# One sum of squares for the final norm of the first block and the first norm of the second, and sums of squares added on GpSimd

## The reference

```python
def rmsnorm(x, g):
    y = x * lax.rsqrt(jnp.mean(x * x, axis=-1, keepdims=True) + EPS)
    return y * g

def first_block(x, ...):
    x = hybrid_layer(x, ...)        # h2 = rmsnorm(x, ln2_g) ahead of its feed-forward part
    return rmsnorm(x, final_g)

def second_block(x, ...):           # rms_norm is the same with NORM_EPS = 1e-5
    h = rms_norm(x, attn_norm_g)
    u = h @ w_in                    # pool part, q, k, v
    ...
    x = x + concat(y_pool, y_diff) @ w_out
    x = x + cross_attention(rms_norm(x, xattn_norm_g), rms_norm(mem, mem_norm_g), ...)
    x = x + moe_ffn(rms_norm(x, ffn_norm_g), ...)       # 32 experts, 4 for a token
    return rms_norm(x, final_norm_g)
```

## Time and profile before

| | |
|---|---|
| median of three runs | 1805.38 us (1804.46 to 1809.14) |
| the profiled execution | 1811.86 us, span 1810.1 us |
| TensorE busy | 1655.3 us, 91% |
| VectorE busy | 733.7 us, 41% |
| ScalarE busy | 482.6 us, 27% |
| GpSimd busy | 153.9 us, 9% |
| DMA, mean over the span | 291 GB/s |
| mean granted clock of TensorE | 0.98 |

### The profile page before, as it was taken

How to read it: one execution, slowest core, us unless ns; L and a number is a source line. 1 busy time by engine, 2 the same in 40 slices (tenths; PEclk the granted TensorE clock), 3 DMA queues, 4 the chain that set the end, 5 groups by cost and what they waited for, 6 DMA issues and landing times.

```text
span 1810.1 us, 22958 instructions
## 1 busy us (share of the span) xinstructions
PE 1655.3 (91%) x9878; PEld 1045.7 (58%) x9878; DVE 733.7 (41%) x1260; ACT 482.6 (27%) x820; POOL 153.9 (9%) x190
## 2 busy tenths in 40 slices
PE   7999999989999899998999988888888888888885
PEld 6998888989999898987333322232323232323221
DVE  5667754677887466745122111111112121212122
ACT  4344454546554344443011000000001010101001
POOL 1200000321552004001000000000000000000000
PEclk9999999999999999999999999999999999999998
DMA  7653322545665452665899999999999999999995
GB/s 203 187 186 106 106 93 93 164 144 171 184 185 180 155 174 78 206 219 189 319 424 422 425 422 424 424 424 423 424 424 425 423 425 424 424 424 425 424 424 230
DMA packets 210202, 525.98 MB, mean 291 GB/s; under 512 B 18121, under 2 KB 135806, under 8 KB 177326
## 3 DMA queue, kind: packets, MB, share of 16 engines
q1 hardware_dynamic: 207104, 519.41, 74.4%
q0 software_dynamic: 2448, 4.82, 1.1%
q10 hardware_dynamic: 542, 0.21, 0.0%
HBM read 523.31 MB, written 1.07 MB: 290 GB/s over the span
## 4 chain that ended last, share of the span: by engine, by line
PE 58%; DMA 35%; DVE 4%; ACT 2%; issue 1%; SPq 0%; POOL 0%; ACTq 0%; DVEq 0%
PE bank L594 57%; DMA slot_ring<-in_w_down 13%; DMA slot_memx<-in_w_down 8%; DMA slot_late<-in_w_down 5%; DMA slot_high<-in_w_down 5%; DMA slot_late<-in_w_gu 1%; DMA slot_last<-in_w_gu 1%; DMA slot_high<-in_w_gu 1%; DVE slot_ring_r L1861 1%; DMA slot_ring<-in_w_in 1%; PE bank L1111 1%; DVE rstd L1900 0%; DVE rot_tmp L2243 0%; ACT high_r L1444 0%; DVE x_sb L1869 0%
## 5 line engine op out<-in xcount | busy, mean ns | idle before, releaser
L594 PE MATMUL bank<-h_hi_r,high_r 128*128 128x256 f32 x1000 | 288.2, 288 | 4.3 <-DVE h_lo_r L1861 4.3
L1861 DVE TENSOR_TENSOR slot_ring_r<-slot_ring,high_r 128x1024 fp32r<-128x1024 f32 x198 | 244.9, 1280 | 101.6 <-ACT high_r L1444 99.3
L594 PE MATMUL bank<-h_lo_r,high_r 128*128 128x256 f32 x1000 | 285.6, 286 | 0.0
L594 PE MATMUL bank<-h_hi_r,slot_ring_r 128*128 128x256 f32 x952 | 271.8, 285 | 0.0
L1865 DVE TENSOR_SCALAR ga<-bank 128x512 f32<-128x512 f32 x32 | 22.1, 692 | 585.1 <-PE bank L594 585.1
L1444 ACT ACTIVATE high_r<-slot_ring 128x1024 fp32r<-128x1024 f32 x198 | 198.0, 1053 | 61.7 <-PE bank L594 43.4
L594 PEld LDWEIGHTS bank<-h_hi_r,high_r 128*128 128x128 f32 x1000 | 193.6, 194 | 5.2 <-DVE h_lo_r L1861 5.0
L594 PEld LDWEIGHTS bank<-h_lo_r,high_r 128*128 128x128 f32 x1000 | 194.0, 194 | 0.1
L1444 ACT ACTIVATE th_e<-ga 128x512 f32<-128x512 f32 x32 | 20.2, 630 | 620.9 <-DVE ga L1865 620.9
L594 PEld LDWEIGHTS bank<-h_hi_r,slot_ring_r 128*128 128x128 f32 x952 | 184.5, 194 | 0.0
L594 PE MATMUL bank<-slot_ring,xg 128*64 128x512 f32 x528 | 124.8, 604 | 12.1 <-DMA slot_ring<-in_w_gu 12.1
(11 more groups left out here) (410 smaller groups left out, 2955.9 us busy)
## 6 DMA issues: line engine op xcount, KB each, us to landing
slot_ring<-in_w_gu SPq DMA_DIRECT2D x66, 1024.0 KB, 22.0
slot_high<-in_w_gu SPq DMA_DIRECT2D x50, 1024.0 KB, 22.1
slot_ring<-in_w_down SPq DMA_DIRECT2D x49, 1024.0 KB, 22.6
slot_last<-in_w_gu SPq DMA_DIRECT2D x38, 1024.0 KB, 22.3
slot_ring<-in_w_in SPq DMA_DIRECT2D x36, 1024.0 KB, 5.0
slot_late<-in_w_gu SPq DMA_DIRECT2D x32, 1024.0 KB, 22.0
slot_high<-in_w_down SPq DMA_DIRECT2D x25, 1024.0 KB, 23.3
slot_ring<-in_w_up SPq DMA_DIRECT2D x44, 512.0 KB, 4.7
```

Source lines behind the costliest of these rows:

```text
L594: return e.matmul(o, lhs, rhs, start=start, stop=stop, skip_group_check=True)
L1861: return e.tensor_tensor(o, i, j, op)
```

## The change

The second norm of the pair takes its sum from squares of x with the gain g1 in the scale, and its gain is g1 g2, so it doesn't wait for the final norm. The final norm is done later: its squares behind memory unit 3, added by GpSimd into one tile, its one sum behind uk 1, its root behind memory unit 4, its products behind the splits for upool. In ln2_g, xattn_g and ffn_g GpSimd adds the squares of pieces 1 and 2 onto piece 0, and TensorE sums pieces 0 and 3 only.

```diff
+        eps_col = {EPS1: small("eps1", 1), EPS2: small("eps2", 1), EPS1 * EPS2: small("eps12", 1)}
+        gain12, gain_sq = small("gain12", KT), small("gain_sq", KT)
...
+        x_sq = tiles(at("x_sq", MIX + (KT + BT) * S, KT * S), KT)
...
...
@@ tensor_program
                 q.wait_ge(*sq_by(norm, i)["square", norm, i])
+                if norm in ADDED:
+                    q.wait_ge(*pool["squares", norm])
...
             def add_residual(w, src, ready, norm):
                 for i in range(4):
                     project((w, i), src, ready, (dve, ("residual", w, i)))
-                    if i:
-                        sums(norm, h, i - 1)
+                sums(norm, h, 0)
                 sums(norm, h, 3)
...
-            pe.mark("final start")
-            for i in range(4):
-                sums("final_g", h, i)
+            pe.mark("block2")
             memory_unit(2)
-            pe.mark("block2")
             for i in range(4):
                 sums("attn_g", h, i)
             memory_unit(3)
...
                 project(("uk", i), hs, h_of("attn_g"), (dve, ("uk", i)))
                 if i:
+                    banks.take(q, ("final_g", "sums"))
+                    q.wait_ge(*pool["squares", "final_g"])
+                    matmul(bank(("final_g", "sums"))[:, 0:S], ones, x_sq[:, 0, :], True, True).then_inc(*pe.step("sums", "final_g"))
+                    banks.give(("final_g", "sums"), (act, ("root", "final_g")))
                     memory_unit(4)
...
+            project(("out2", 2), mix_s, mix_ready, (dve, ("residual", "out2", 2)))
+            project(("out2", 3), mix_s, mix_ready, (dve, ("residual", "out2", 3)))
             sums("xattn_g", h, 0)
-            project(("out2", 2), mix_s, mix_ready, (dve, ("residual", "out2", 2)))
-            sums("xattn_g", h, 1)
-            project(("out2", 3), mix_s, mix_ready, (dve, ("residual", "out2", 3)))
-            sums("xattn_g", h, 2)
             sums("xattn_g", h, 3)
...
@@ gpsimd_program
+            def add_squares(norm):
+                for i in (1, 2):
+                    for j in (0, i):
+                        q.wait_ge(*(act if j % 2 else dve)["square", norm, j])
+                    q.wait_ge(*pool.last())
+                    e.tensor_tensor(h[:, 0:2, :], h[:, 0:2, :], h[:, 2 * i:2 * i + 2, :], ALU.add).then_inc(
+                        *pool.step("squares", norm))
...
             after_all(q, "block2")
+            q.wait_ge(*act["square", "final_g", 3])
+            for n in (4, 2, 1):
+                q.wait_ge(*pool.last())
+                e.tensor_tensor(x_sq[:, 0:n, :], x_sq[:, 0:n, :], x_sq[:, n:2 * n, :], ALU.add).then_inc(
+                    *pool.step("squares", "final_g"))
             q.wait_ge(*dve["pool zero"])
...
             pool.mark("ffn start")
+            add_squares("ffn_g")
+            q.wait_ge(*pool["squares", "ffn_g"])
             for c in range(2):
...
@@ scalar_program
             round_h("ln1_g")
+            q.wait_ge(*dve["gain squares"])
+            af(gain_sq, gain_sq, ACT.Sqrt).then_inc(*act.step("gain root"))
...
-            act.mark("final start")
-            after_all(q, "final start")
-            for i in range(4):
-                squares("final_g", h, x, i, dve["residual", "down", i])
-            sqrt_table()
-            root("final_g", EPS1, "ln2_g")
-            memory_unit(2)
             act.mark("block2")
             after_all(q, "block2")
+            sqrt_table()
             for i in range(4):
-                squares("attn_g", h, x, i, dve["h", "final_g", 2 * i + 1])
-            sqrt_table()
-            root("attn_g", EPS2, "final_g")
+                q.wait_ge(*dve["residual", "down", i])
+                for k in (2 * i, 2 * i + 1):
+                    af(h[:, k, :], x[:, k, :], ACT.Square, scale=gain_sq[:, k:k + 1]).then_inc(*act.step("square", "attn_g", i))
+            memory_unit(2)
+            root("attn_g", EPS1 * EPS2, "ln2_g")
             round_h("attn_g")
             memory_unit(3)
+            for i in range(4):
+                squares("final_g", x_sq, x, i, dve["residual", "down", i])
             for i in range(2):
                 ahead(("uq", i))
                 evac(("uq", i), uq[:, 2 * i:2 * i + 2, :], two_of(("uq", i)), ("uq", i), HD ** -0.5)
                 ahead(("uk", i))
                 if i:
                     memory_unit(4)
+            root("final_g", EPS1, "attn_g")
...
@@ vector_program
             apply("ln1_g", x, h, hs.lo)
+            g1, g2 = (cols_sb[:, col_at[n]:col_at[n] + KT] for n in ("final_g", "attn_g"))
+            tt(gain12, g1, g2, ALU.mult).then_inc(*dve.step())
+            tt(gain_sq, g1, g1, ALU.mult).then_inc(*dve.step())
+            own()
+            ts(gain_sq, gain_sq, EPS2, ALU.add, 1.0 / D, ALU.mult).then_inc(*dve.step("gain squares"))
...
-            dve.mark("final start")
-            q.wait_ge(*act["square", "final_g", 3])
-            apply("final_g", x, x)
-            memory_unit(2)
             dve.mark("block2")
             after_all(q, "block2")
-            q.wait_ge(*act["square", "attn_g", 3])
-            apply("attn_g", x, h, hs.lo)
+            memory_unit(2)
+            apply("attn_g", x, h, hs.lo, gain=gain12)
             memory_unit(3)
...
             for i in range(2):
                 ahead(("upool", i))
+            q.wait_ge(*act["square", "final_g", 3])
+            apply("final_g", x, x)
             for t in two:
                 e.memset(t[:, 0:16], 0.0).then_inc(*dve.step("pool zero"))
```

More of the change, by code:

```diff
@@ L309, in hybrid_moe_program @@
         spare, half_b = small("spare", 1), small("half_b", 32)
-        eps_col = {EPS1: small("eps1", 1), EPS2: small("eps2", 1)}
+        eps_col = {EPS1: small("eps1", 1), EPS2: small("eps2", 1), EPS1 * EPS2: small("eps12", 1)}
+        gain12, gain_sq = small("gain12", KT), small("gain_sq", KT)
         FORGET = sm_at[0]
@@ L399, in hybrid_moe_program @@
         dprob = [area(f"dprob{i}", 384) for i in range(DIFF_H)]
+        assert (DIFF_H + 2) * 384 >= KT * S
+        x_sq = tiles(at("x_sq", MIX + (KT + BT) * S, KT * S), KT)
         assert free[0] <= AR + AREAS - 5 * SLOT
@@ L570, in hybrid_moe_program @@
         MEM_STEPS = ((0, 1), (2, 3), (4, 5), (6, 7), ())
+        ADDED = ("ln2_g", "xattn_g", "ffn_g")
         NORM_START = {"ln2_g": "ln2 start", "xattn_g": "xattn start", "ffn_g": "ffn start"}
@@ L587, in sq_by @@
         def sq_by(norm, i):
-            return act if i % 2 or norm in ("mem_g", "final_g", "attn_g") else dve
+            return act if i % 2 or norm in ("mem_g", "attn_g") else dve
         def tensor_program(e):
@@ L1369, in gpsimd_program @@
             pool.mark("ln2 start")
+            add_squares("ln2_g")
             pool.mark("ff start")
@@ L1380, in gpsimd_program @@
                 ff_split(i)
-            pool.mark("final start")
             pool.mark("block2")
             after_all(q, "block2")
+            q.wait_ge(*act["square", "final_g", 3])
[3 more added lines that the diff above has]
+                    *pool.step("squares", "final_g"))
             q.wait_ge(*dve["pool zero"])
@@ L1405, in gpsimd_program @@
             pool.mark("xattn start")
+            add_squares("xattn_g")
             pool.mark("cross start")
@@ L1894, in squares, with apply @@
                     ALU.mult).then_inc(*dve.step("square", norm, i))
-            def apply(norm, src, dst, lo=None, steps=None):
+            def apply(norm, src, dst, lo=None, steps=None, gain=None):
                 for k in range(KT + 2) if steps is None else steps:
@@ L1902, in apply @@
                     if k < KT:
-                        stt(dst[:, k, :], src[:, k, :], col(norm, k), rstd, ALU.mult, ALU.mult).then_inc(*dve.step("h", norm, k))
+                        stt(dst[:, k, :], src[:, k, :], col(norm, k) if gain is None else gain[:, k:k + 1], rstd, ALU.mult, ALU.mult).then_inc(*dve.step("h", norm, k))
                     if lo is not None and k >= 2:
@@ L1914, in vector_program @@
                 evac(("x", i), x[:, 2 * i:2 * i + 2, :], two_of(("x", i)), ("x", i))
-            for eps in (EPS1, EPS2):
+            for eps in eps_col:
                 e.memset(eps_col[eps], eps).then_inc(*dve.step("eps"))
```

## The result

The changed kernel takes 1796.8 us (median of 5 runs, 1794.4 to 1797.4), the kernel before 1808.6 in the same series (5 runs, 1804.5 to 1813.5): a ratio of 0.9929, interval 0.991 to 0.9947. In a second series they were 1795.6 and 1809.0, 0.9932 [0.9911, 0.9953]. The difference of the medians is 11.9 and 13.4 us where 9.4 was forecast; the profiled span fell by 14.5. (The median of 1805.4 before, from which the forecast counted, came from three runs.)

The account below looks back on a forecast made before the run. Ahead of the expert stage's weight transfers the chain is nearly all TensorE, so instructions taken off it count. 13.7 + 4.8 - 0.5 - 5.2 - 1.8 - 1.6 = 9.4 us gained, 1805.4 to 1796.0; range 1788 to 1803.

Parts of the forecast that it names:

- The join, 28.4 to 14.6: Between block one and two: one sum, two TensorE gaps and a low clock removed; 13.8 us gained, rounded to 13.7.
- under 3 us at clock 1.0: Sign in the join: after down and the memory unit, one sum of 16 taking under 3 us at clock 1.0.
- The later h: At the join's end: h being ready later costs TensorE 0.2 us, taken off the gain.
- The three norms, 4.8: ln2_g, xattn_g, ffn_g: two of four groups of sums dropped each, 5.1 us, cut to 4.8 by collisions in xattn_g.
- The rotation, 5.2 late: Rotation of uk on TensorE waits for ScalarE's squares and VectorE splits taking turns with GpSimd's adds: 5.2 us lost.
- Rival 1: Engines hardly block each other: stall 1.2, no clock drop, softmax 0.8 late; 16.6 us gained, 1788.8. Chance 0.17.
- The low clock, 1.8: After the gap ahead of uk's rotation, TensorE at about half clock for 3.6 us: 1.8 us lost.
- The new sum, 0.5: The final norm's new sum of 2 instructions on TensorE, 0.3 and the slow start: 0.5 us lost.
- The softmax, 1.6 late: VectorE's final-norm reciprocal and products ahead of the first maximum delay the softmax: 1.6 us lost, bounds 0 and 3.5.
- Rival 2: Upper-end costs: softmax 3.5 late, squares 4.4, low clock twice as long; 4.7 us gained, 1800.7. Chance 0.2.
- Rival 3: Expert stage gives back part through differently timed slots; half of 9.4 kept is 1800.7, none 1805.4. Chance 0.1.
- Rival 4: Slower: GpSimd's bias subtractions move behind ffn_g's adds and delay the experts, if 6.7 us each slower by 5.4. Chance 0.05.

Follow-up runs that it names:

- the experiment in which TensorE sums all: Changed kernel without GpSimd's adds of the final norm's squares, TensorE summing 8 products instead of 2: 1798.6 us, 0.9929.
- the pair of experiments: Changed kernel with GpSimd's three final-norm adds held until uk 1 is rotated: 1790.8 us; with ScalarE's four squares moved behind uq 1's split too: 1791.1 us.
- the profile with the wait filled: Changed kernel with 12 float32 matmuls on constants between the rotations of uq 0 and uk 0, output not read: 1794.4 us, 0.9924.
- the reciprocal put on top: Changed kernel with one more VectorE reciprocal (1.75 us) behind the final norm's products, ahead of the softmax: 1798.5 us, 0.9936.
- the squares later: Changed kernel with ScalarE's four final-norm squares moved behind the split of uq 1, GpSimd's adds moving too: 1791.1 us, in another series 1789.8.
- the adds later: Changed kernel with GpSimd's three final-norm adds waiting until VectorE has rotated uk 1, ScalarE's squares staying: 1790.8 us, 0.990.

## Why the prediction was right

**The join, 28.4 to 14.6.** Measured 28.42 to 14.75. From the end of down: squares begin after 4.04 us (4.15 forecast), take 3.29 (2.8), the sum ends after 8.8 (8.6), the reciprocal begins after 10.7 (10.2), uq 0 after 14.75 (14.45, from the prediction's own 615.15 and 629.6; its 14.6 has part of the 0.2 in it that is then taken off once more, and the 13.7 is right to 0.1). ScalarE after, for the earlier trace rows:

```profile
614.34 1.28 ACT L1466 ACT_TABLE_LOAD   x1 [6.33 <-DVE x_sb L1891]
615.74 3.29 ACT L1466 ACTIVATE h_sb<-x_sb,gain_sq 128x256 f32<-128x256 f32 x8
618.94 1.99 ACT L1466 ACTIVATE high_r<-slot_ring 128x1024 fp32r<-128x1024 f32 x2
621.30 0.45 ACT L1466 ACTIVATE rstd<-bank,eps 128x256 f32<-128x256 f32 x1
```

The 8 squares with the gain column as scale take 0.41 each, where four without took 0.35; the half microsecond more didn't count. TensorE has no gap from the end of down to uq 0: the 14.75 are two memory units and the sum of 16 between them. That sum misses its sign, "under 3 us at clock 1.0": it took 3.27 at 1.00, for the reason given with the experiment in which TensorE sums all. So the sum was under-priced by 0.5; the memory unit ahead of it was over 0.2 sooner than counted, which hid part of that. The later h was too small at 0.2: uq 0 and uk 0 take 0.8 longer.

**The three norms, 4.8.** 1.6, 1.6 and 1.7: 4.9, each group gone being worth about the 0.85 of the earlier trace rows. In xattn_g TensorE waits 0.91 for the last residual's squares. Of that, 0.58 stands in each norm, before as after; the 0.33 is new, for 0.6 forecast, and it comes about as forecast: GpSimd's second add takes 2.21 instead of 1.3 and VectorE's two half splits beside it 3.45 instead of 2.35, and the last residual stands behind them. That norm gave 1.63, for 1.4 forecast.

**The rotation, 5.2 late.** 4.75 measured, 17.0 us from uq 0 for 17.4 forecast. Its parts moved against each other. Without turns the forecast had 1.2 and 0.2 for the later h, the runs 1.8 (1.0 and 0.8). GpSimd's turns were put at 4.0, and are 3.0. Rival 1 is refuted by the pair of experiments: the four splits take 7.72 beside the adds and 4.74 without. How strict the turns are is seen by addition. From the first add at 634.18 to the end of the last split at 642.71 are 8.53 us; less 4.74 of splits, 3.8 remain for the three adds, where 4.6 was counted from 1.29 for 512. By the page "GPSIMD Engine Reference" of the Trainium skill, section 3.1, they would be an estimated 3.9; here the page was nearer than the row of 128x512. The 3.0 us that went with the adds, and the 2.68 of the first split beside the first add, agree with the exclusive lock of the shared port that the page "SBUF — State Buffer" of the Trainium skill has in section "Who interferes with whom".

**The low clock, 1.8.** 1.7, of which 1.15 show up by uq 1 alone; 1.6 to 2.2 over four profiles with this wait. In the profile with the wait filled it is gone.

**The new sum, 0.5.** 0.45.

**The softmax, 1.6 late: the term that was mis-sized.** It is 0.15. The start was nearly right: VectorE takes the first maximum 1.1 us later against dscores (3.26 behind the first one, 2.20 before), 1.3 forecast. The step "products took 0.72 while it ran and 0.35 after, about 1 us for a head" failed. From the first maximum on, the four heads took 6.07, 5.91, 5.86 and 5.23, where before they took 6.72, 6.22, 5.23 and 5.22: 23.1 together for 23.4. The third head, now beside GpSimd's pooling, does pay for it, but 0.6 and not 1. The first two stand beside the pooling in both kernels, and yet they pay 1.0 less than before. Of that, 0.45 is a wait of VectorE for TensorE ahead of the first head's second maximum, which is gone because VectorE begins later. The other 0.5 is in the products of the two heads, which meet other instructions of the pooling than before; the stage has its 34.4 in eight of the profiles with the join, so it isn't chance, but no experiment took it apart. So the heads end 0.7 late, where 2.3 were forecast (how 2.3 and idle times of 0.47 and 1.22 make 1.6 the prediction doesn't show). Behind them ScalarE's idle time of 0.47 took the larger part; its last bank of uv is only 0.15 late:

```profile
705.59 0.60 ACT L1466 ACTIVATE uv<-bank 128x512 f32<-128x512 f32 x1
708.69 2.36 DVE L1883 TENSOR_TENSOR slot_ring_r<-slot_ring,high_r 128x1024 fp32r<-128x1024 f32 x2 [0.64 <-ACT high_r L1466]
```

The bound of 3.5 was not idle: the reciprocal put on top went through at full length.

**Sum.** 13.7 + 4.9 - 4.75 - 1.7 - 0.45 - 0.15 = 11.5, where 9.4 was forecast; 1.45 of the 2.1 is the softmax, the rest the stall and the norms, a few tenths each. The difference of the medians, 11.9, fits it; the 13.4 of the second series would have room for the router's 1.0 as well. That 1796.0 was forecast and 1796.8 measured is in part luck: the kernel before came out at 1808.6, 3.3 us above the 1805.4 that the forecast started from, and that made up for the larger gain.

**The other rivals.** Rival 2 (upper ends) had the squares at 4.4 and the softmax at 3.5; neither came. Rival 3: from the experts' begin to the end of the span are 951.3 us before and 951.1 after, so the stage kept nothing. Rival 4: the bias subtractions take 1.3 each, not 2.0. They end at 826.3, and GpSimd then idles 6.7 us until VectorE's h is there, so they stayed under the cover.

**What stays open.** Why down's 1636 matmuls take 195.5 in some profiles and 194.1 in others (a pitch of 0.1191 and 0.1182 us), why ckv 0 begins anywhere in 6 us, and whether the router's 1.0 belongs to ffn_g, wasn't settled. Nor was it tried to shorten ScalarE's queue in the join. The 14.75 can't gain by it, since TensorE has no gap there; the 0.8 in uq 0 and the wait of the rotation, to which the chain runs over ScalarE and VectorE alone, could.

## What to carry to other kernels

When work is moved off the engine that bounds a stretch, look for the one place where it is put into a full queue, and price it there: here 4.75 us of stall and 1.7 of low clock behind it took a third of what the join and the norms gave, and one wait that puts GpSimd's adds behind VectorE's splits gave most of it back. When collisions are moved, count them over all the heads, before and after: here one head more beside GpSimd cost 0.6, and the stage as a whole 0.15. And before a change of the clock in one profile is put down to an edit, look at the same wait in profiles of kernels without that edit: here the clock stayed up in two of eleven with no filler at all.

## What the runs showed that was not expected

A small instruction of VectorE can wait for a whole long one of GpSimd: with the squares later, the 128x256 add of the rotation, which stands beside GpSimd's 128x1024 add (640.33 to 642.73), took 2.22 us, where the other adds of the rotation take 0.42.

```profile
640.79 2.22 DVE L1884 TENSOR_TENSOR uk<-uk,rot_tmp 128x256 f32<-128x256 f32 x1
```

It cost nothing measurable there: TensorE was already on uq 1, and the stage took 30.78 for 30.80 with the adds later.

The same idle stretch doesn't always bring the clock down. Ahead of the router TensorE waits 3.1 us in every profile without fillers there. In one it was then granted 1.00 and fell one stretch later, in the others it fell within or behind this wait, three times for 6.8 us instead of 3.4. The stage has 18.55, 19.1 and 19.9 to 20.1 us accordingly, and the cross attention 53.7 to 56.9. So a difference of one profile of 1 to 2 us in such a stage says nothing by itself.
